# First attention layer: the causal mask moves from TensorE's products to the scan's second table and to products on GpSimd

## The reference

```python
strict = key_pos[None, :] < qpos[:, None]
z = jnp.einsum('bhqd,bhkd->bhqk', qb, kh).astype(jnp.float32) * scale
log_stay = jnp.where(strict, jax.nn.log_sigmoid(-z), 0.0)
log_after = lax.cumsum(log_stay, axis=3, reverse=True) - log_stay
w = jnp.where(strict, jnp.exp(jax.nn.log_sigmoid(z) + log_after), 0.0)
return jnp.einsum('bhqk,bhkd->bhqd', w, vh.astype(jnp.float32)).astype(q.dtype)
```

## Time and profile before

| | us |
|---|---|
| median of 3 runs (2042.55 to 2044.46) | 2043.62 |
| the profiled execution | 2042.31 |
| its span | 2040.5 |
| TensorE busy (matmuls) | 2012.2 |
| VectorE busy | 1068.5 |
| ScalarE busy | 798.5 |
| GpSimd busy | 630.6 |

### The profile page before, as it was taken

How to read it: one execution, slowest core, us unless ns; L and a number is a source line. 1 busy time by engine, 2 the same in 40 slices (tenths; PEclk the granted TensorE clock), 3 DMA queues, 4 the chain that set the end, 5 groups by cost and what they waited for, 6 DMA issues and landing times.

```text
span 2040.5 us, 28707 instructions
## 1 busy us (share of the span) xinstructions
PE 2012.2 (99%) x9556; PEld 1643.5 (81%) x9556; DVE 1068.5 (52%) x1445; ACT 798.5 (39%) x1182; POOL 630.6 (31%) x416
## 2 busy tenths in 40 slices
PE   7999999999999999999999999999999999999997
PEld 5777888888887777788888888888888888888886
DVE  6666644343366666544343456699854552332324
ACT  5544444342254455444342254222227343223124
POOL 1111255341134333345340254444444031001013
PEclk9999999999999999999999999999999999999999
DMA  4122245443334434245443332233232323233333
GB/s 155 63 64 90 83 139 171 163 145 94 102 112 95 93 82 103 83 139 191 146 143 93 99 118 83 93 95 100 93 100 87 101 84 101 93 101 94 94 102 103
DMA packets 64037, 218.82 MB, mean 107 GB/s; under 512 B 7792, under 2 KB 9968, under 8 KB 63856
## 3 DMA queue, kind: packets, MB, share of 16 engines
q1 hardware_dynamic: 60912, 213.96, 32.9%
q0 software_dynamic: 3072, 4.20, 1.7%
HBM read 211.83 MB, written 2.10 MB: 105 GB/s over the span
## 4 chain that ended last, share of the span: by engine, by line
PE 93%; DVE 2%; issue 2%; ACT 1%; POOL 1%; DMA 1%; SPq 0%; DVEq 0%; POOLq 0%; ACTq 0%
PE G L1524 28%; PE G L1526 28%; PE G L1525 28%; PE Z L1648 2%; PE Z L1629 2%; PE O L1666 1%; PE Z L1524 1%; PE Z L1526 1%; PE Z L1525 1%; POOL qkv L1381 1%; PE O L1675 0%; DVE Z L1053 0%; DMA raw<-stream 0%; POOL ql L1371 0%; POOL kl L1371 0%
## 5 line engine op out<-in xcount | busy, mean ns | idle before, releaser
L375 ACT ACTIVATE wh<-raw 128x1024 fp32r<-128x1024 f32 x338 | 358.6, 1061 | 963.2 <-PE G L1526 950.8
L1524 PE MATMUL G<-xh,wh 128*128 128x512 f32 (+1 forms) x1616 | 633.4, 392 | 10.8 <-DVE xl L835 9.2
L1526 PE MATMUL G<-xh,wl 128*128 128x512 f32 (+1 forms) x1616 | 626.9, 388 | 0.0
L1525 PE MATMUL G<-xl,wh 128*128 128x512 f32 (+1 forms) x1616 | 626.9, 388 | 0.0
L806 DVE TENSOR_TENSOR wl<-raw,wh 128x1024 fp32r<-128x1024 f32 x277 | 388.4, 1402 | 183.6 <-ACT wh L375 180.4
L1524 PEld LDWEIGHTS G<-xh,wh 128*128 128x128 f32 x1616 | 303.9, 188 | 83.7 <-issue 16.9
L1526 PEld LDWEIGHTS G<-xh,wl 128*128 128x128 f32 x1616 | 303.8, 188 | 62.7
L1525 PEld LDWEIGHTS G<-xl,wh 128*128 128x128 f32 x1616 | 304.0, 188 | 61.6 <-issue 1.0
L1524 PE MATMUL G<-yh,wh 128*128 128x512 f32 x904 | 351.9, 389 | 0.3 <-DVE wl L806 0.3
L1526 PE MATMUL G<-yh,wl 128*128 128x512 f32 x904 | 350.6, 388 | 0.0
L1525 PE MATMUL G<-yl,wh 128*128 128x512 f32 x904 | 350.5, 388 | 0.0
(11 more groups left out here) (245 smaller groups left out, 1965.8 us busy)
## 6 DMA issues: line engine op xcount, KB each, us to landing
raw<-stream SPq DMA_DIRECT2D x340, 512.0 KB, 3.5
araw<-ada_w SPq DMA_DIRECT2D x48, 512.0 KB, 4.3
fraw<-stream SPq DMA_DIRECT2D x8, 512.0 KB, 4.4
qkv<-tmp POOLq DMA_DIRECT2D x64, 64.0 KB, 3.4
h<-x_t SPq DMA_DIRECT2D x8, 256.0 KB, 6.4
out_t<-h SPq DMA_DIRECT2D x16, 128.0 KB, 1.8
con<-const_d SPq DMA_DIRECT2D x1, 1344.0 KB, 9.8
cs<-c_row SPq DMA_DIRECT2D x1, 512.0 KB, 4.3
```

Source lines behind the costliest of these rows:

```text
L375: eng.activation(wh[s][:, :, :], raw[s][:, :, :], ACT.Copy).then_inc(w_hi, 1)
L1524: eng.matmul(total, hi[:, k, :], src_h[:, k, cols], start=k == 0, stop=False)
L1525: eng.matmul(total, hi[:, k, :], src_l[:, k, cols], start=False, stop=False)
L1526: mm = eng.matmul(total, lo[:, k, :], src_h[:, k, cols], start=False, stop=k == kt - 1)
```

## The change

The mask leaves TensorE. Its eight products in front of the scores are gone, with their tables `idb` and `maskb`, the two copies that made these and the semaphore `consts`; the first score product of a bank now opens it. Instead:

- The constants get a row table of 512 columns at the end of `con`: 0, and in the last 128 columns 1 from the diagonal on. VectorE's scan takes the larger of the running product and this table (`ALU.max`, read backwards as before), where it used to multiply by a column of ones. Inside the masked part the state is 1.
- GpSimd multiplies the diagonal blocks of `ez` by a table of 0 and 1 (`C_KEEP`), in one product for each bank (`keep_a`, new semaphore `kept`): 256 elements a partition for banks 0, 1 and 2, 128 for banks 3 and 4. VectorE's takes wait for `kept` and no longer for `take_ready`.
- The first two loads of the loop on SyncE are written out, and the row table comes by its own DMA of 256 KB behind them. VectorE waits for it (`in_open`) once, before attention. `con` itself is otherwise loaded as before.

```diff
-C_ID, C_ONE, C_MASK, C_COS, C_SIN, C_COUNT = 0, 128, 256, 384, 896, 1408
-C_ALL = C_COUNT + TRI
+C_ID, C_ONE, C_KEEP, C_COS, C_SIN, C_COUNT = 0, 128, 256, 384, 896, 1408
+C_OPEN = C_COUNT + TRI
+C_ALL = C_OPEN + SEQ
...
     t[:, C_ONE:C_ONE + P] = 1.0
-    t[:, C_MASK:C_MASK + P] = np.where(j < i, 0.0, NEG)
+    t[:, C_KEEP:C_KEEP + P] = j < i
+    t[:, C_ALL - P:C_ALL] = j >= i
     freq = (np.float32(10000.0) ** (-np.arange(0, HD, 2, dtype=np.float32) / np.float32(HD))).astype(np.float32)
...
-            at = 1
+            load(1, 0)
+            load(1, 1)
+            eng.dma_start(con[:, C_OPEN:], const_d[:, C_OPEN:]).then_inc(in_open, 16)
+            at = 2
             for which in range(2):
...
                             part = stay[:, c, o:o + w][:, ::-1]
-                            eng.tensor_tensor_scan(part, part, ones[:, 0:1].to_broadcast([P, w]), 1.0, ALU.mult,
-                                                   ALU.mult).then_inc(left, 1)
+                            eng.tensor_tensor_scan(part, part, con[:, C_ALL - w:C_ALL][:, ::-1], 1.0, ALU.mult,
+                                                   ALU.max).then_inc(left, 1)
...
-                        eng.wait_ge(take_ready, BANKS * a + c + 1)
+                        eng.wait_ge(kept, BANKS * a + c + 1)
                         eng.wait_ge(left, 2 * NB * a + (2, 4, 6, 7, 8)[c])
...
                                   ALU.add).then_inc(sq_added, 2 if n == KD - 1 else 1)
-            eng.wait_ge(in_con, 16)
-            for dst, c in ((idb, C_ID), (maskb, C_MASK)):
-                eng.tensor_copy(dst[:, :], con[:, c:c + P]).then_inc(consts, 1)
+            eng.wait_ge(in_open, 16)
             attention(0)
...
+                    def keep_a(c):
+
+                        eng.wait_ge(take_ready, BANKS * a + c + 1)
+                        if c < 2:
+                            seen = ez[:, c, 2 * BLK:].rearrange("p (m j) -> p m j", m=2)
+                        elif c == 2:
+                            seen = ez[:, c, :].rearrange("p (m n j) -> p m n j", m=2, n=2)[:, :, 1, :]
+                        else:
+                            seen = ez[:, c, 3 * BLK:].rearrange("p (m j) -> p m j", m=1)
+                        below = con[:, C_KEEP:C_KEEP + P].rearrange("p (m j) -> p m j", m=1)
+                        eng.tensor_tensor(seen, seen, below.to_broadcast([P, 2 if c < 3 else 1, P]),
+                                          ALU.mult).then_inc(kept, 1)
+
                     if layer == 0:
+                        if attn:
+                            for c in range(BANKS):
+                                keep_a(c)
                         if gemm:
...
-                    def masks():
-
-                        for c, places in enumerate(((256, 384), (256, 384), (128, 384), (384,), (384,))):
-                            for m, o in enumerate(places):
-                                eng.matmul(Z[c][:, o:o + BLK], idb[:, :], maskb[:, :], start=m == 0, stop=False,
-                                           skip_group_check=True)
-
                     def scores():
                         eng.wait_ge(qk_lo, 2 * gp)
-                        if layer == 0:
-                            masks()
                         st, mv = (qh, ql), (kh, kl)
...
                         product(1, 0, xh, xl, x_lo, 0, bank=FIRST_V)
-                        eng.wait_ge(consts, 2)
                         eng.wait_ge(evac[0], 2)
```

More of the change, by code:

```diff
@@ L151, in build_program @@
         vec = sb("vec", [P, V_ALL])
-        idb, maskb = sb("idb", [P, P], BF16), sb("maskb", [P, P], BF16)
         rstd = sb("rstd", [P, SEQ])
@@ L197, in build_program @@
         O = ctx.enter_context(nc.psum_tensor("O", [P, SEQ], F32))
-        in_vec, in_con = sem("in_vec"), sem("in_con")
+        in_vec, in_con, in_open = sem("in_vec"), sem("in_con"), sem("in_open")
         in_h = [sem(f"in_h{n}") for n in range(KD)]
@@ L205, in build_program @@
         evac = [sem("evac0"), sem("evac1")]
-        consts = sem("consts")
         cs_ready = sem("cs_ready")
@@ L224, in build_program @@
         stay_ready, take_ready = sem("stay_ready"), sem("take_ready")
-        left, taken = sem("left"), sem("taken")
+        kept, left, taken = sem("kept"), sem("left"), sem("taken")
         pv_done = sem("pv_done")
@@ L298, in _ @@
                     load(0, 1)
-            eng.dma_start(con[:, :], const_d).then_inc(in_con, 16)
+            eng.dma_start(con[:, 0:C_OPEN], const_d[:, 0:C_OPEN]).then_inc(in_con, 16)
             def load_ada(j, s):
@@ L1627, in scores @@
                                         eng.wait_ge(half_bank, gp)
-                                    first = layer == 1 and x == 0 and y == 0 and (b < 2 or (b, hh) == (2, 0))
+                                    first = x == 0 and y == 0 and (b < 2 or (b, hh) == (2, 0))
                                     mm = eng.matmul(Z[c][:, o:o + w], st[x][rows, blk], mv[y][rows, cols], start=first,
```

## The result

The changed kernel takes 2059.12 us (median of 4 runs, 2057.64 to 2060.07), beside 2043.61 for the kernel before on the same chip: ratio 1.0075, 95% interval 1.0062 to 1.0087. That is 15.5 us more, where 11.0 were forecast. The profiled execution took 2057.64 us, the shortest of the four, with a span of 2055.5, so 15.0 us more of span.

A forecast was written before the change was run, and what follows sets the result against it. TensorE was taken as the bound, with VectorE's chain close behind in the first attention layer. Opening slot 1.5, six middle slots 7.8 and last 1.7 gave +11.0 us, on the 2043.62 median about 2054.5 us; range 2047 to 2064.

The forecast's parts named there:

- S: Growth of VectorE's chain per first-layer attention slot from being pushed back by five GpSimd products: 1.8 us.
- The bound and the rooms: First attention layer: TensorE bounds, VectorE close behind; longer chain unfelt up to 0 (opening), 0.50 (middle), 0.12 us (last slot).
- The opening slot gains 0.3: Opening slot of the first attention layer: its chain starts from the scores, so removing masks gains 0.3 us in full.
- The sum: First attention layer's loss: opening slot 1.5, six middle slots 7.8, last slot 1.7; together +11.0 us.
- The expected wait in front of L1648: Middle slots: TensorE idles 1.3 us before the first turned weights, waiting for VectorE's take.
- Both move together, so no second wait: Bank 4's take ends 1.86 us after bank 3's; TensorE has 3.2 us of work between turned-weight rounds.
- Second layer unchanged: Second layer and FFN, behind the edited first attention layer: no change in time.
- Rival 1: First-layer slots: scans do not contend with GpSimd, so not slower, 2040 to 2043.5 us; chance 0.12.
- Rival 3: VectorE's scan with a real table and maximum runs at the take's rate: faster, 2038.5 to 2040.5 us; chance 0.03.
- Rival 2: First-layer slots: dear GpSimd products lengthen VectorE's chain by 3.2 us a slot, ending at 2065.6 us; chance 0.05.
- The sign: GpSimd products over 1 us at 256 wide where VectorE stands waiting would show they are dear.
- the main case: All five GpSimd products push VectorE back, by 1.1 to 2.9 us a slot: 2049 to 2063 us; chance 0.80.

The follow-up runs named there:

- Without products: The changed kernel without GpSimd's five products a slot, diagonal blocks unmasked, takes waiting for `take_ready`: 2040.37 us, ratio 0.9987 to the kernel before.
- the select: The changed kernel with GpSimd's products replaced by a select by position that reads one SBUF input, same widths: 2044.71 us, ratio 1.0006 to the kernel before.
- the identity: The changed kernel with an identity table in the scan, started from 0; GpSimd only clears each strip's last column: 2042.37 us, ratio 0.9996 to the kernel before.
- the products aside: The changed kernel with its five GpSimd products on tables into an idle tile, mask's zeroes left out, no take waiting: 2058.47 us, ratio 1.008 to the kernel before.
- masks and products: The kernel before, TensorE's mask products kept, plus five GpSimd products a slot on tables into an idle tile: 2057.96 us, ratio 1.0071.
- the last one free: The changed kernel without GpSimd's products in the last of the eight slots, diagonal blocks unmasked there: 2054.97 us, ratio 1.0059 to the kernel before.

## Why the prediction was right, point by point

The mechanism was the forecast one, and the size was low: 11.0 us forecast, 15.0 in the profile. Of the 4.0 us between them, 1.7 come from the eight slots, above all from a larger S, 1.6 from a fall of the clock that the prediction did not have, and 0.6 from the second layer.

- **The bound and the rooms** held. With S = 2.0, opening slot, middle slots and last slot lose S less 0.43, 0.46 and 0.09, against 0.3, 0.50 and 0.12 in the sum. "The opening slot gains 0.3" was low. VectorE's first scans there, before and after:

```profile
34.76 2.44 DVE L906 TENSOR_TENSOR_SCAN stay<-stay,con 128x384 f32<-128x384 f32 x4 [2.25 <-ACT stay L466]
...
34.35 3.93 DVE L909 TENSOR_TENSOR_SCAN stay<-stay,con 128x384 f32<-128x384 f32 x4 [1.79 <-ACT stay L469]
```

They start 0.41 us earlier, and 0.46 counted from the product on `ssum` (21.47 and 21.52), so that is what the masks were worth. Without products a middle slot follows at 23.99 instead of 24.44 us, so there it is 0.455, towards the upper bound of 0.55.
- **S = 1.8** was 2.0. The wide products cost 0.50 and not 0.47, the narrow ones 0.245 and not 0.19: the line through two widths was too low at its narrow end. In six middle slots this is 1.2 of the 1.4 us by which they exceed 7.8.
- **The sum** was 11.0 for the first layer; up to the turned weights of the last slot it measured 12.7. The expected wait in front of L1648 was 1.3 us and read 1.83. TensorE also idles where the masks stood: with them the wait is 1.33. By the prediction's own account, in which a middle slot's mask gain is only a wait moved, the expected figure had to be 1.3 + 0.3 = 1.6.
- **"Both move together, so no second wait"** held as a wait, but the step missed that a longer idle time lets the clock fall: 1.64 us, the largest single miss.
- **"Second layer unchanged"** is 0.6 us off: the waits for the low part of k are 2.8 us in all instead of 1.7. They differ in every kernel (1.6 with the select, 3.0 with the identity). They hang on the transfers that swap halves of k, and no run here settles what delays these.
- **Rival 1** (scans don't contend) fell: scans of 128 read 895 ns instead of 398. **Rival 3** fell: a scan of 512 takes 1.211 us with a maximum and 1.215 with a product. **Rival 2** fell by S, which is 2.0 and not 3.2. The sign that the prediction named for it did come: GpSimd's products of 256 read over 1 us.

```profile
L1395 POOL TENSOR_TENSOR ez<-ez,con 128x256 f32<-128x256 f32 x24 | 27.7, 1175 | 36.1 <-ACT ez L470 36.0
```

But that is their time beside VectorE, in which they wait too, so the sign could not tell rival 2 from the main case. The start is as forecast, without a wait for `in_open`: VectorE's weight split starts at 21.30 us with no idle time before it.

## What to carry to other kernels

Work that is moved from a full engine to an idle one was not free here, because the idle one held up the engine that is the next bound. Measure the room behind the bound first (here 0.50 us a slot), and price the move as instructions times their push on the neighbour, not by their own duration. And before an idle TensorE is counted at its length, look at the granted clock behind waits of two microseconds: each such fall cost another 1.3 to 1.6 us here. In the second layer a longer wait and the fall behind it together hid most of what an edit had gained 400 us earlier.

## What the runs showed of the hardware

- GpSimd and VectorE: a product with two SBUF inputs pushes a chain of scans and takes back by 0.50 us at 256 wide (if the pushes add up) and 0.245 at 128; a select with one input by 0.16 at 256 wide and 0.07 at 128; a memset of one or two columns by nothing. The Trainium skill (SBUF — State Buffer, SBUF: two separate sides) has a GpSimd instruction that reads SBUF hold the shared pair of ports for its whole length against a VectorE instruction with two SBUF inputs. For the products the trace agrees that the two hold each other up, though a push of 0.50 is less than the 0.748 us that such a product takes alone; for the select, 0.709 us long and nearly free, it does not agree.
- The clock: it fell behind idle times of TensorE of 2.02 us (no products, second layer), 2.17 (the last slot, both in the changed kernel and with the products aside), 2.66 (opening slot, masks and products) and 2.84 (identity, second layer). It did not behind 1.83 (six times) or 2.63 us (opening slot of the changed kernel) nor 2.66 (the same slot with the last one free). Length alone doesn't decide.
